# A two-block transformer with experts on one core: another front, router and branch order, and the second pair's up matrices in halves

## What is computed

```python
def first_block(...):
    h = rms_norm(x, attn_pre_g)
    proj = einsum("bsd,de->bse", h, w_in)
    q_a, k_a, v_a, q_b, k_b, v_b = split(proj, IN_SPLITS)
    y_a = rms_norm(swa_sink_attention(q_a, k_a, v_a, swa_sinks, swa_slopes), swa_out_g)
...
def _hierarchical_moe(h, w_group, w_expert, w_gate, w_up, w_down):
    group_prob = softmax(h @ w_group)
    group = argmax(group_prob)
    exp_logits = (h @ w_expert).reshape(n, N_GROUPS, EXPERTS_PER_GROUP)
    exp_logits = take_along_axis(exp_logits, group)
    top_p, top_local = top_k(softmax(exp_logits), TOP_K)
    top_p = top_p / sum(top_p)
    weight = group_gate * top_p
...
        return (silu(xb @ w_gate[e]) * (xb @ w_up[e])) @ w_down[e]
```

## Time and profile before

| | us |
|---|---|
| three runs | 1000.51, 1000.73, 1002.49 |
| median | 1000.73 |
| the profiled execution | 1001.55 |
| its span in the trace | 999.9 |
| PE busy | 973.4 (97%) |
| DVE busy | 550.0 (55%) |
| ACT busy | 346.4 (35%) |
| data moved | 312.21 MB, mean 312 GB/s |

### The profile page before, as it was taken

The page is one execution under the profiler, slowest core; times in us unless marked ns, Lnnn a source line. Parts: engine busy times, 40 slices in busy tenths (PEclk is TensorE's granted clock), DMA queues, the critical chain, the costliest instruction groups (busy, mean ns, idle before and its releaser), DMA issues.

```text
span 999.9 us, 15776 instructions
## 1 busy us (share of the span) xinstructions
PE 973.4 (97%) x6129; PEld 672.9 (67%) x6137; DVE 550.0 (55%) x1051; ACT 346.4 (35%) x579; POOL 96.6 (10%) x139
## 2 busy tenths in 40 slices
PE   8999999999999999999999999999999999989896
PEld 6998799999999997989765544445444444433433
DVE  6478689889999998758426322422222222222222
ACT  4665675444454464546332111111111110111102
POOL 8200101011111200200001000600000000000000
PEclk9999999999999999999999999999999999999999
DMA  8424467888789745444938999999999999999995
GB/s 306 170 85 169 153 223 260 290 316 313 285 300 358 275 169 188 148 169 169 391 114 274 380 401 402 417 430 426 427 429 426 427 427 429 428 427 430 430 417 210
DMA packets 61979, 312.21 MB, mean 312 GB/s; under 512 B 4285, under 2 KB 5674, under 8 KB 49130
## 3 DMA queue, kind: packets, MB, share of 16 engines
q1 hardware_dynamic: 54112, 284.83, 71.2%
q0 software_dynamic: 7392, 26.54, 7.5%
q10 hardware_dynamic: 426, 0.16, 0.1%
HBM read 310.47 MB, written 1.05 MB: 312 GB/s over the span
## 4 chain that ended last, share of the span: by engine, by line
PE 77%; DMA 11%; DVE 7%; issue 2%; ACT 2%; POOL 0%; SPq 0%; DVEq 0%; ACTq 0%
PE bank L972 10%; PE bank L1538 10%; PE bank L974 10%; PE bank L973 10%; PE bank L1557 10%; PE bank L1592 8%; DMA eslots<-in_w_gate 8%; PE bank L1459 4%; PE bank L1119 3%; DVE ring_r L2049 2%; PE bank L1469 2%; DMA ring<-in_w_in 2%; PE bank L1047 1%; DMA ring<-in_w_up 1%; PE bank L1085 1%
## 5 line engine op out<-in xcount | busy, mean ns | idle before, releaser
L972 PE MATMUL bank<-hT_r,ring_r 128*128 128x256 f32 x664 | 189.4, 285 | 1.4 <-DVE ring_r L2049 1.3
L974 PE MATMUL bank<-hT_r,ring_r 128*128 128x256 f32 x664 | 187.9, 283 | 0.0
L2049 DVE TENSOR_TENSOR ring_r<-ring,ring_r 128x2048 fp32r<-128x2048 f32 (+1 forms) x74 | 164.6, 2258 | 13.9 <-ACT ring_r L1677 13.6
L1677 ACT ACTIVATE ring_r<-ring 128x2048 fp32r<-128x2048 f32 (+1 forms) x74 | 136.5, 1890 | 42.6 <-DMA ring<-in_w_up 34.6
L973 PE MATMUL bank<-v_tok_r,ring_r 128*128 128x256 f32 x496 | 140.4, 283 | 0.0
L972 PEld LDWEIGHTS bank<-hT_r,ring_r 128*128 128x128 f32 x664 | 127.4, 192 | 2.4 <-DVE ring_r L2049 1.6
L974 PEld LDWEIGHTS bank<-hT_r,ring_r 128*128 128x128 f32 x664 | 127.4, 192 | 0.0
L1592 PE MATMUL bank<-eslots,scratch 128*64 128x512 f32 x496 | 113.4, 595 | 0.7 <-ACT scratch L1929 0.7
L973 PEld LDWEIGHTS bank<-v_tok_r,ring_r 128*128 128x128 f32 x496 | 95.2, 192 | 0.2
L974 PE MATMUL bank<-ring_r,hn_r 128*128 128x512 f32 (+2 forms) x220 | 80.4, 365 | 0.0
L1592 PEld LDWEIGHTS bank<-eslots,scratch 128*64 128x64 f32 x496 | 35.7, 137 | 62.9 <-issue 61.0
(11 more groups left out here) (359 smaller groups left out, 1598.7 us busy)
## 6 DMA issues: line engine op xcount, KB each, us to landing
eslots<-in_w_gate SPq DMA_DIRECT2D x28, 2048.0 KB, 23.7
eslots<-in_w_up SPq DMA_DIRECT2D x28, 2048.0 KB, 23.5
eslots<-in_w_down SPq DMA_DIRECT2D x27, 2048.0 KB, 27.1
ring<-in_w_up SPq DMA_DIRECT2D x16, 2048.0 KB, 11.8
ring<-in_w_in SPq DMA_DIRECT2D x9, 2048.0 KB, 7.9
ring<-in_w_down SPq DMA_DIRECT2D x8, 2048.0 KB, 9.0
kT<-in_w_ada POOLq DMA_DIRECT2D x24, 512.0 KB, 7.6
ring<-in_w_out SPq DMA_DIRECT2D x4, 2048.0 KB, 9.0
```

What stands on the lines that cost most here:

```text
L972: pe.matmul(dst, lhs[0], rhs[0], start=start, stop=False, **flags)
L974: return pe.matmul(dst, lhs[1], rhs[0], start=False, stop=stop, **flags)
L1677: sc.activation(hi, raw, ACT.Copy).then_inc(s_whi, 1)
L2049: last = ve.tensor_tensor(lo, raw, hi, ALU.subtract)
```

## The change

Four parts.

1. **Front.** The twelve `stage` loads (L1637 to L1644 before) go to SP's queue, between chunks 1 and 2. The first half of chunk 0 is loaded and split in two quarters (`first_quarter`), with the semaphore `s_whi_first` for the first. The wake-up matmuls ahead of the first turn go, and of three ahead of the second, one is left. "ka" is computed by `project_rounded_first`, with all products of the rounded weights first. "v" becomes "vT": 128 x 256 in the orientation of the queries, and an item "turn" of two transposes brings it to the tokens' orientation. ACT takes the items 0 to 3 before it rounds chunk 2, DVE does its weight residuals ahead of its items within the attention. The first product with the values waits for the turned copy.
2. **Router.** The best and the second best expert are found in every group at once, beside the search for the best group; the group's choice is multiplied in afterwards. `lgT` lies in another buffer (`eact`) and its halves are copied by DVE and ACT. The last residual product stands behind the ranks, the wake-up matmuls are fewer, and the ranks are written as places at once (`iota` starts at 1), without the step of `slots(0)`.
3. **Order of the branches.** The body for more than 16 pairs now stands ahead of the body for 16.
4. **Halves.** `matrix(1, 3)` and `matrix(1, 2)` are loaded in halves, the second halves first: that of `(1, 3)` without a wait, that of `(1, 2)` when the first tile of the input is written, the first halves when the whole matrices were loaded before.

```diff
-        items1 += [(1, "ka", (0, 0)), (1, "v", (P, P, 0))]
+        items1 += [(1, "ka", (0, 0)), (1, "vT", (P, 0))]
...
-        items1 += [q_item(0), k_item(0), q_item(1), k_item(1), q_item(2), q_item(3), k_item(2), k_item(3), v_item(0),
+        items1 += [q_item(0), (1, "turn", (0, 0)), k_item(0), q_item(1), k_item(1), q_item(2), q_item(3), k_item(2), k_item(3), v_item(0),
...
-        BETWEEN = [{0: [7], 1: [8], 2: [9], 3: [10], 4: [11], 5: [12], 6: [13], 7: [14], 8: [15]},
+        V_TURNED = 7
+        BETWEEN = [{0: [7, 8], 1: [9], 2: [10], 3: [11], 4: [12], 5: [13], 6: [14], 7: [15], 8: [16]},
...
+            if kind == "vT":
+                return [(PT[:, 0, 0:S], bank[:, 0:S])]
+            if kind == "turn":
+                return [(vt[:, :, 0:P], bank[:, 0:S].rearrange("p (t n) -> p t n", t=T))]
...
+            for first, end, done in ((0, 2, s_loaded_once), (2, 4, loaded[SLOT_N + 3]), (4, KD, loaded[0])):
+                sp.dma_start(raw[:, first:end, :], w_in[:, first:end, 0:HALF]).then_inc(done, 16)
+            straight(N_IN + 1, w_in[:, :, HALF:2 * HALF])
+            cw = a["conv_w"].rearrange("o j (f p) -> (o j f) p", p=P)
...
+            sp.dma_start(stage[:, 0, :], cw[0:P, :]).then_inc(s_stage, 16)
+            sp.dma_start(stage[0:FT, 1, :], cw[P:P + FT, :]).then_inc(s_stage, 16)
...
+                sp.dma_start(stage[row:row + v.shape[0], 2, :], v).then_inc(s_stage, 16)
+            straight(N_IN + 2, w_in[:, :, 2 * HALF:3 * HALF])
...
-            into(SLOT_N + 2, matrix(1, 2), (s_back, 4))
+            part_into(SLOT_N + 3, matrix(1, 3), 1, 2)
+            sp.wait_ge(s_hT["moe"], 1)
+            part_into(SLOT_N + 2, matrix(1, 2), 1, 2)
+            sp.wait_ge(s_back, 4)
+            part_into(SLOT_N + 2, matrix(1, 2), 0, 2)
             sp.wait_ge(s_r1, 1)
             sp.dma_start(final_row, a["g_final_2"].partition_broadcast(P)).then_inc(s_vectors, 16)
-            into(SLOT_N + 3, matrix(1, 3), (s_acc, 1))
+            sp.wait_ge(s_acc, 1)
+            part_into(SLOT_N + 3, matrix(1, 3), 0, 2)
...
+                if kind == "turn":
+                    piece_taken(blk, AHEAD[0])
+                    for t in range(T):
+                        last = pe.transpose(bank[:, t * P:(t + 1) * P], PT[:, 0, t * P:(t + 1) * P], ident[:, :])
+                    last.then_inc(s_gemm[blk], 1)
+                    return
...
-                    if kind in ("q", "k", "ka"):
+                    if kind in ("q", "k", "ka", "vT"):
...
-            stay_awake(PS[7], 6)
             turn("attn1", hn, range(T - 1))
-            stay_awake(PS[6], 3)
+            stay_awake(PS[6], 1)
...
-                pe.wait_ge(s_whi, 1)
-                rounded_products(first, 0)
-                pe.wait_ge(s_wlo_first, 1)
-                rounded_products(first, 1)
+                quarters = (range(2), range(2, 4))
+                for ks, rounded_part in zip(quarters, (s_whi_first, s_whi)):
+                    pe.wait_ge(rounded_part, 1)
+                    rounded_products(ks, 0)
+                for n, ks in enumerate(quarters):
+                    pe.wait_ge(s_wlo_first, n + 1)
+                    rounded_products(ks, 1)
...
+            def project_rounded_first(n):
+                c, kind, (c0, _) = items1[n]
+                assert kind == "ka" and n < AHEAD[0]
+                w = split_view((N_IN + c) % LANES)
+                dst = item_bank(0, n)[:, 0:S]
+                pe.wait_ge(s_whi, 2 * (N_IN + c) + 2)
+                for k in range(KD):
+                    for part in range(2):
+                        pe.matmul(dst, w[0][:, k, c0:c0 + P], tiles("attn1", k)[part],
+                                  start=(k == 0 and part == 0), stop=False)
+                split_ready(N_IN + c)
+                for k in range(KD):
+                    last = pe.matmul(dst, w[1][:, k, c0:c0 + P], tiles("attn1", k)[0], start=False,
+                                     stop=(k == KD - 1))
+                last.then_inc(s_gemm[0], 1)
             pe.wait_ge(s_vec, 1)
             project_first(4)
             turn_gains()
-            for n in range(4, AHEAD[0] + 1):
+            project_rounded_first(4)
+            for n in range(5, AHEAD[0] + 1):
...
-            pe.wait_ge(s_lgT, 1)
+            pe.wait_ge(s_lgT, 2)
...
-            for b in range(2 * T):
+            def residual(b):
                 t, c = b // 2, b % 2
                 pe.wait_ge(s_h2, b + 1)
-                last = pe.matmul(PS[b][:, :], ident[:, :], x[:, t, c * HALF:(c + 1) * HALF], start=True, stop=False,
+                return pe.matmul(PS[b][:, :], ident[:, :], x[:, t, c * HALF:(c + 1) * HALF], start=True, stop=False,
                                  skip_group_check=True)
-            last.then_inc(s_acc, 1)
-            stay_awake(PS[4], 1)
+            for b in range(2 * T - 1):
+                residual(b)
             pe.wait_ge(s_A, 1)
             rk = PS[7]
             pe.matmul(rk[:, 0:2 * NEXP], before[:, :], Aa.rearrange("p t n -> p (t n)"), start=True, stop=False)
             for t in range(T):
                 last = pe.matmul(PS[6][:, 0:NEXP], ones[:, :], Aa[:, t, :], start=(t == 0), stop=(t == T - 1))
             last.then_inc(s_rank, 1)
+            residual(2 * T - 1).then_inc(s_acc, 1)
...
-            stay_awake(PS[4], 4)
+            stay_awake(PS[4], 1)
...
-            with pe.If(n_pairs < PAIRS + 1):
-                pair(PAIRS - 1, PAIRS - 1, last_one=True)
-                combine_last(PAIRS - 1)
             with pe.If(n_pairs > PAIRS):
                 pair(PAIRS - 1, PAIRS - 1, last_one=True)
                 combine_last(PAIRS - 1)
                 with pe.Fori(PAIRS, PAIRS * PASSES) as p:
                     pair(p, None)
                     combine(p)
+            with pe.If(n_pairs < PAIRS + 1):
+                pair(PAIRS - 1, PAIRS - 1, last_one=True)
+                combine_last(PAIRS - 1)
...
-            split_one(N_IN, 0)
+            for quarter, (done, ready) in enumerate(((s_loaded_once, s_whi_first), (loaded[SLOT_N + 3], s_whi))):
+                sc.wait_ge(done, 16)
+                raw, hi, _ = first_quarter(quarter)
+                sc.activation(hi, raw, ACT.Copy).then_inc(ready, 1)
...
             split(N_IN + 1)
+            take(0, range(4))
             split(N_IN + 2)
             sc.wait_ge(s_lamx, 1)
             sc.activation(lam2, lam2, ACT.Exp).then_inc(s_lame, 1)
-            take(0, range(AHEAD[0] + 1))
+            take(0, range(4, AHEAD[0] + 1))
...
+            sc.wait_ge(s_lg, 1)
+            sc.activation(lgT[1], PS[4][64:64 + NL, 0:S], ACT.Copy).then_inc(s_lgT, 1)
...
-            for half in range(2):
-                last = ve.tensor_copy(lgT[half], PS[4][64 * half:64 * half + NL, 0:S])
-            last.then_inc(s_lgT, 1)
+            ve.tensor_copy(lgT[0], PS[4][0:NL, 0:S]).then_inc(s_lgT, 1)
...
-            then(ve.tensor_reduce(gmax, groups, X, ALU.max))
+            experts = by_group(lg[:, :, NGRP:NL])
+            ve.tensor_reduce(gmax, groups, X, ALU.max)
+            then(ve.tensor_reduce(m1, experts, X, ALU.max))
+            for t in range(T):
+                ve.scalar_tensor_tensor(gfirst[:, t, :], groups[:, t, :], gmax[:, t:t + 1], frac[:, 0:NGRP], ALU.is_lt,
+                                        ALU.add)
+            then(ve.tensor_tensor(by_group(first), experts, in_group(m1), ALU.is_lt))
+            ve.tensor_reduce(gidx, gfirst, X, ALU.min)
+            then(ve.tensor_tensor(first, first, both_tiles(frac), ALU.add))
             ve.tensor_scalar(ngmax, gmax, -1.0, None, ALU.mult).then_inc(s_r1, 1)
-            first_largest(groups, gmax, gfirst)
-            then(ve.tensor_reduce(gidx, gfirst, X, ALU.min))
+            then(ve.tensor_reduce(i1, by_group(first), X, ALU.min))
             for t in range(T):
-                last = ve.tensor_scalar(outside[:, t, :], frac[:, 0:NGRP], gidx[:, t:t + 1], NEG, ALU.not_equal, ALU.mult)
-            then(last)
...
-            then(ve.tensor_reduce(i2, first, X, ALU.min))
-            then(one_hot(A2, i2))
+                ve.tensor_scalar(inside[:, t, :], frac[:, 0:NGRP], gidx[:, t:t + 1], None, ALU.is_equal)
+            then(ve.tensor_tensor(by_group(A1), by_group(both_tiles(frac)), in_group(i1), ALU.is_equal))
+            then(ve.scalar_tensor_tensor(by_group(el2), by_group(A1), 2 * NEG, experts, ALU.mult, ALU.add))
+            ve.tensor_tensor(by_group(A1), by_group(A1), in_group(inside), ALU.mult)
+            then(ve.tensor_reduce(m2, by_group(el2), X, ALU.max))
+            ve.scalar_tensor_tensor(by_group(places_in), in_group(inside), -1.0, by_group(both_tiles(frac)), ALU.mult,
+                                    ALU.add)
+            then(ve.tensor_tensor(by_group(first), by_group(el2), in_group(m2), ALU.is_lt))
+            ve.tensor_tensor(m2, m2, m1, ALU.subtract)
+            then(ve.tensor_tensor(first, first, places_in, ALU.add))
```

(6 more changed lines are left out.)

99 lines of the change are left out of this document (40 added, 59 removed).

## The result

The changed kernel takes 1009.57 us (median of 4 runs, 1007.74 to 1010.18), the kernel before beside it 1001.53 us (4 runs): ratio 1.0074, 95% interval 1.0062 to 1.0087. It is 8.0 us slower, where 3.3 us faster was forecast. The profiled execution took 1007.74 us, its span is 1005.9 us, against 1001.55 and 999.9 before: 6.0 us of span. It is the shortest of its four, so the profile shows somewhat less than the whole loss.

A forecast was written before the change was run, and what follows sets the result against it. PE was taken to bound the kernel, also setting when the saturated weight loads start. Terms -1.2 - 2.1 - 0.8 + 0 + 0.8 = -3.3 us gave 998.2 profiled, 997.4 us as median; range 995.0 to 1000.4.

The forecast's parts named there:

- Front, first product: Kernel start: input rounded sooner, so PE's first product starts 0.9 us earlier, and a 0.3 us wait goes: -1.2 us.
- Front, value item: Front: value item computed transposed takes 2.95 us instead of 5.33, less 0.26 for turning it back: -2.1 us.
- Router: Expert assignment before PE's gather: 11 dependent steps instead of 17, 4.3 us instead of 4.92, plus the later stage: -0.8 us.
- The later stage: Router, ahead of the one-hot rows: DVE loses its first step and decides, not PE: -0.23 us.
- Halves: Second pair's up matrices loaded in halves at about 541 to 551 us: same bytes, dry DMA place follows, 0 us.
- Branch order: Loop's end: the 3.69 us jump now stands ahead of the last pair, leaving 0.6 us idle plus 0.2 pipeline: +0.8 us.
- The lead of 3.1 us: At the last pair: PE's sequencer reaches the branch test at 962.7, its gate product starts at 965.84, hiding 3.1 us.
- the bound, 2.5 us more: Jump ahead of the last pair: upper end of its cost, since it now stands in full DMA traffic, some 2.5 us more.
- all instants up to 540 us earlier by that: Expected sign: first attention products 3.3 us earlier, and everything up to 540 us earlier by the same amount.
- a rule about the current prefetch window: PE's jumps: a taken branch to a target outside the prefetched window forces a DMA fetch before the engine goes on.
- Rival D: Last pair: the jump's fetch waits behind weight loads and the clock falls; slower, about 1005.4 us at a 10 us jump; chance 0.05.
- rival C: Late gate-weight waits: DMA decides, front and router gains only lengthen waits at 878.86 and 937.68; about 1001.5 us; chance 0.08.

The follow-up runs named there:

- the version with everything in place: The changed kernel with PE's two branch bodies in the old order and 56 always-met wait instructions spread over pairs 1 to 4: 999.21 us, ratio 0.9971.
- with the loop misplaced: The changed kernel with only PE's two branch bodies put back in the old order: 1000.67 us, ratio 0.9987 to the kernel before.
- with the jump ahead of the last pair: The changed kernel, new branch order, with 56 more PE instructions in the branch body that never runs: 1004.69 us, ratio 1.0029.
- with its target at a bad place: The changed kernel run once more, unchanged: 1010.15 us, ratio 1.0073 to the kernel before.
- the version with the moved last pair: The changed kernel, new branch order, with 56 never-executed PE instructions that move only the last pair's place: 1004.69 us, ratio 1.0029.

## Why the prediction was wrong

The loss is put together from four kernels: the version with everything in place 999.2 us, with the loop misplaced 1000.7 (+1.5), with the jump ahead of the last pair 1004.7 (+4.0), with its target at a bad place 1010.15 (+5.5). The four stand in two groups of runs, whose kernels before are at 1002.42 and 1002.52. The +4.0 goes across the groups and holds two edits, the order and the 56 instructions that never run; the order alone, within one group, cost 3.2 us with the loop in place and 2.6 us in the kernel before. So the +5.5 is measured, the jump costs 2.6 to 4.0, and the +1.5 is within the noise.

- **Front, first product (-1.2).** Right: 0.97 us earlier in the changed kernel's trace, and no wait ahead of "ka".
- **Front, value item (-2.1).** Right in place and size: the attention was 3.75 us earlier where 3.3 was forecast for both front terms, and against the old item in the same version it was 2.7 and 2.3 us earlier (32.31 and 34.98; 32.41 and 34.72). From there on single executions scatter: at 385 us the traces with the new item lie between 2.1 and 4.5 us ahead of the kernel before, but the second one of the changed kernel lies 0.8 us behind it.
- **Router (-0.8).** Right in size: the chain went from 4.92 to 4.17 us (in 12 dependent steps, not the 11 of the prediction), and the gather came 0.6 us earlier beyond what the chain's start had gained (4.27 us). The later stage, priced at -0.23, gave nothing (+0.12): the moved residual product took 1.10 us instead of some 0.4, so that PE decided there and not DVE.
- **Halves (0).** Right, to about 1 us.
- **Branch order (+0.8).** This step failed. The lead of 3.1 us was right (a jump of 6.10 us left 3.08 idle), and three things were wrong. The jump was priced at 3.69 us from a row that stands where no weights are loaded; in full traffic it takes 5.95 to 6.20 us in all five executions that have it. The text named the bound, 2.5 us more, and took the lower end. Then, the price ended with the idle time plus 0.2 us for an emptied pipeline, which no row shows, while the clock fell to half: the 3.1 us of idle cost 4.6 us. I had that row, the gate of 8.78 us after an idle of 2.70 us, and used it only for a rival. And the second stall, behind the target, was in no case; it is the largest part of the loss, 5.5 us.
- **Not costed at all: what was taken out moved the loop.** The prediction said "all instants up to 540 us earlier by that", and counted the removed instructions only as time. It held the jumps back for safe at 0.2 us because the loop is not edited. It also took the jumps of 3.69 and 0.2 us as agreeing with a rule about the current prefetch window, and did not ask how wide the window must be. The short jump agrees only if the window is wider than the loop: it goes back over some 1635 PE instructions without a fetch. Rival D came nearest (a slower result through the jump in full traffic), but its deciding point, a jump of 7.3 us, was never reached: the jump took 6.1 us. The kernel lost through the second stall, the clock and the other jump.
- **The clean gain.** With both jumps cured the change gives 2.9 us, where the terms without the branch add up to 4.1; the interval reaches from 1.7 to 4.2, so the difference is hardly clear of noise. The profile has a place for it: PE waits 7.6 us for gate weights instead of 6.95 before, and 1.75 us for the last up and down matrices instead of nothing. That is rival C in a weaker form, and it is argued from one execution.
- **The range.** The terms' ends add up to -5.2 and +1.6 (with 3.3 for the jump at its bound), not to -5.1 and +0.7. The measured +8.0 lies outside either.

The Trainium skill ("Runtime: NRT & Kernel Launch", "Instruction fetch mechanics") says that PE holds 2048 instructions, refilled in blocks of 16 KiB or 256 instructions. The traces agree with the block: their packets have 16 KB, and the second stall at the jump back moved as block ends 256 instructions apart would have it. By the traces the loop's round has 1634 to 1636 PE instructions, which with those numbers is 6.4 blocks: it lies in 7 or 8 blocks by its place, and fits beside a block fetched ahead only if it lies in 7. The runs agree with that count (counted from the old place, 0, -7, -10 and +57 instructions fit, -63 and +200 don't, and these last two differ by about one block), but no run shows the capacity itself; that part is argued, not shown.

## What to carry to other kernels

An instruction that is removed can move a loop across the border of what the engine holds of its program. Before and after each change to a kernel with a large loop (here some 1635 PE instructions), look at the length of its jump back and at the packets of the instruction queue; if they changed, move the loop by a few dozen idle instructions where the engine has slack before judging the change. And leave the likely path of a branch at the end of a loop the one that falls through: a jump far ahead is paid where it stands, at the prices of the traffic and of the clock that may fall in its idle time. The last is not certain: behind idle times of 2.7 us for gate weights the next gate took 8.78 us in some places and 7.09 in others, and 7.09 even behind one of 3.24 us (the version with the moved last pair, at 935.76), with the granted clock at 1.00; behind the jump ahead of the last pair the product was slow in all five executions.

## What the runs showed that I had not expected

- A jump back over the whole loop took 0.217 us in all eight profiled executions in which the loop fitted and 6.1 to 6.4 us in all five in which it did not, at nearly the same time and with the DMA's share at 1.00 in both.
- 56 instructions that are never executed made the kernel 5.5 us faster.
- All 18 long jumps ended 1.3 to 1.5 us after a packet of instructions had landed; in full DMA traffic that packet started some 2.6 us later than without.
- The jump over the long body takes 3.35 to 3.98 us behind the last loads (eight executions) and 5.95 to 6.20 us in front of them (five).
